# Adding the halves of the value blocks by accumulating transfers, and taking the hidden product in two halves

## What is computed

```python
def swiglu(x, w_in, w_out):
    gate, up = jnp.split(x @ w_in, 2, axis=-1)     # 1024 -> 2 x 2816
    return (jax.nn.silu(gate) * up) @ w_out        # 2816 -> 1024
```

## Time and profile before

| | |
|---|---|
| median of 3 runs | 966.76 us (966.62 to 968.57) |
| the profiled execution's own time | 964.49 us |
| its span, first to last instruction | 962.8 us |
| PE, PEld busy | 99%, 84% of the span |
| DVE, ACT, POOL busy | 88%, 64%, 11% |
| mean granted TensorE clock | 0.998 of full speed |
| DMA, mean over the span | 205 GB/s; SP's queue 55.3%, POOL's 11.1% of the 16 engines |
| chain that ended last | PE 91%, DVE 5%, ACT 2% |

### The profile page before, as it was taken

The page is one execution under the profiler, slowest core; times in us unless marked ns, Lnnn a source line. Parts: engine busy times, 40 slices in busy tenths (PEclk is TensorE's granted clock), DMA queues, the critical chain, the costliest instruction groups (busy, mean ns, idle before and its releaser), DMA issues.

```text
span 962.8 us, 13790 instructions
## 1 busy us (share of the span) xinstructions
PE 952.3 (99%) x4904; PEld 806.8 (84%) x4904; DVE 849.0 (88%) x1174; ACT 620.4 (64%) x727; POOL 108.7 (11%) x146
## 2 busy tenths in 40 slices
PE   9999999999999999999999999999999999999996
PEld 7888888888888888888888888888888888888885
DVE  5999998996898999889889989899898997999886
ACT  6776667436646667675576666549998546667660
POOL 0211111100210111110011101100100100111110
PEclk9999999999999999999999999999999999999999
DMA  9778877753656786876587777935243656786761
GB/s 306 240 228 234 280 235 223 232 178 129 223 180 205 217 244 193 236 227 206 173 237 235 239 231 232 271 124 184 89 131 115 235 192 190 215 242 194 237 162 55
DMA packets 140912, 197.31 MB, mean 205 GB/s; under 512 B 7280, under 2 KB 114336, under 8 KB 140720
## 3 DMA queue, kind: packets, MB, share of 16 engines
q1 hardware_dynamic: 126032, 173.56, 55.3%
q0 software_dynamic: 14256, 22.38, 11.1%
q10 hardware_dynamic: 560, 0.52, 0.2%
HBM read 182.79 MB, written 1.06 MB: 191 GB/s over the span
## 4 chain that ended last, share of the span: by engine, by line
PE 91%; DVE 5%; ACT 2%; issue 1%; DMA 1%; POOL 0%; DVEq 0%; SPq 0%; ACTq 0%
PE psum L2012 23%; PE psum L2026 15%; PE psum L2019 12%; PE psum L1821 12%; PE psum L1830 12%; PE psum L1825 12%; DVE w_lo L995 1%; PE psum L2402 1%; ACT w_hi L503 1%; PE psum L1814 1%; PE psum L2388 1%; DVE w_lo L1031 1%; DMA raw<-in_ffn_w_out 1%; DVE w_lo L1001 1%; PE psum L1996 1%
## 5 line engine op out<-in xcount | busy, mean ns | idle before, releaser
L995 DVE TENSOR_TENSOR w_lo<-raw,w_hi 128x2048 fp32r<-128x2048 f32 x125 | 285.1, 2284 | 20.9 <-ACT w_hi L503 20.8
L2012 PE MATMUL psum<-xT,w_hi 128*128 128x512 f32 x1024 | 254.2, 390 | 0.5
L503 ACT CAST w_hi<-raw 128x2048 fp32r<-128x2048 f32 x125 | 238.3, 1914 | 24.5 <-DMA raw<-in_ffn_w_in 15.0
L2012 PEld LDWEIGHTS psum<-xT,w_hi 128*128 128x128 f32 x1024 | 191.3, 188 | 44.8 <-ACT ffn_tok L573 3.2
L2019 PEld LDWEIGHTS psum<-xT,w_lo 128*128 128x128 f32 x1024 | 139.7, 190 | 10.0
L2019 PE MATMUL psum<-xT,w_lo 128*128 128x256 f32 x1024 | 142.8, 282 | 0.0
L1821 PE MATMUL psum<-w_hi,xT 128*128 128x512 f32 x447 | 128.7, 399 | 0.8 <-DVE arena L1538 0.4
L1830 PE MATMUL psum<-w_hi,xT 128*128 128x512 f32 x447 | 124.8, 390 | 0.2 <-DVE xT L1099 0.2
L1825 PE MATMUL psum<-w_lo,xT 128*128 128x512 f32 x447 | 124.7, 390 | 0.0
L1717 POOL DMA_DIRECT2D ffn_tok<-ffn_tok x64 | 55.0, 859 | 484.7 <-ACT ffn_tok L573 484.7
L1830 PEld LDWEIGHTS psum<-w_hi,xT 128*128 128x128 f32 x447 | 83.9, 188 | 18.3 <-DVE xT L1099 0.5
(11 more groups left out here) (220 smaller groups left out, 1165.3 us busy)
## 6 DMA issues: line engine op xcount, KB each, us to landing
raw<-in_ffn_w_in SPq DMA_DIRECT2D x170, 512.0 KB, 5.2
raw<-in_ffn_w_out SPq DMA_DIRECT2D x88, 512.0 KB, 4.4
raw<-in_c_w_in SPq DMA_DIRECT2D x32, 512.0 KB, 4.7
ffn_tok<-ffn_tok POOLq DMA_DIRECT2D x64, 128.0 KB, 4.9
raw<-in_ab_w_in SPq DMA_DIRECT2D x16, 512.0 KB, 4.9
x_tok<-arena POOLq DMA_DIRECT2D x16, 256.0 KB, 7.3
raw<-in_ab_w_o SPq DMA_DIRECT2D x8, 512.0 KB, 4.2
raw<-in_c_w_o SPq DMA_DIRECT2D x8, 512.0 KB, 4.0
```

Of the source, the lines that this page charges most:

```text
L503: nc.scalar.copy(w_hi[:, slot_of[n]], raw[:, n % RAW]).then_inc(hi_ready, 1)
L995: nc.vector.tensor_tensor(w_lo[:, slot_of[n]], raw[:, n % RAW], w_hi[:, slot_of[n]].bitcast(F32), ALU.subtract).then_inc(lo_ready, 1)
L2012: nc.tensor.matmul(G[0], w_hi[:, slot_of[n + kh], at:at + P], xT_both[:, 4 * kh + k].rearrange("p a s -> p (a s)"), start=kh == k == 0, st ...
```

## The change

`up_add` goes. POOL's `add_gates` becomes `add_halves`: after the transfers for the two gate blocks it issues two more for the value blocks, each once its block is copied out; these have semaphores `value_added[0]` and `value_added[1]`. `up_product` becomes two instructions of 256 columns, one for each block j: it waits for `value_added[j]`. On DVE the first half stays in front of `weight_sums`, the second half and `hidden_sums` come behind them. `hid_product` is two semaphores, so that a copy of block b waits for the half b % 2 alone. On ACT `up_copy(1)` moves ahead of `split_sums_hi` in chunks 4 to 9, and `gates_silu` ahead of `up_copy(3)` in all of them.

```diff
@@ ACT
                 if c > FIRST_FM:
-                    act.wait_ge(hid_product, N_FM * f + c - FIRST_FM)
+                    act.wait_ge(hid_product[b % 2], N_FM * f + c - FIRST_FM)
...
                         hid_early_hi(name, c - 1)
                         hid_late_hi(name, c - 1)
+                        up_copy(name, c, 1)
                         split_sums_hi(name, n)
-                        up_copy(name, c, 1)
                         split_hi(n + 2)
                         up_copy(name, c, 2)
...
                         split_plain_hi(n + 3)
+                    gates_silu(name, c)
                     up_copy(name, c, 3)
-                    gates_silu(name, c)
...
-                act.wait_ge(hid_product, N_FM * (f + 1))
+                for j in range(2):
+                    act.wait_ge(hid_product[j], N_FM * (f + 1))
@@ DVE
-            def up_add(name, c):
-
-                f = SILUS[name]
-                ups = UPS[name]
-                dve.wait_ge(up_copied, 4 * (N_FM * f + c - FIRST_FM + 1))
-                nc.vector.tensor_tensor(ups[:, :, 0:SEQ], ups[:, :, 0:SEQ], ups[:, :, SEQ:], ALU.add
-                                        ).then_inc(up_added, 1)
-
-            def up_product(name, c):
+            def up_product(name, c, j):

                 f = SILUS[name]
-                gates, ups = (a[:, :, 0:SEQ].rearrange("p j (t f) -> p j t f", t=TT) for a in (GATES, UPS[name]))
+                gates, ups = (a[:, j, 0:SEQ].rearrange("p (t f) -> p t f", t=TT) for a in (GATES, UPS[name]))
                 dst = hid_places if c < NC - 2 else hid_blocks[:, 0:512].rearrange("p (j t f) -> p j t f", j=2, t=TT)
                 dve.wait_ge(hidT_lo, NH * f + c)
                 dve.wait_ge(late_lo, N_PROD * f + c)
                 dve.wait_ge(gate_silu, N_FM * f + c - FIRST_FM + 1)
-                dve.wait_ge(up_added, N_FM * f + c - FIRST_FM + 1)
-                nc.vector.tensor_tensor(dst, ups, gates, ALU.mult).then_inc(hid_product, 1)
+                dve.wait_ge(value_added[j], 16 * (N_FM * f + c - FIRST_FM + 1))
+                nc.vector.tensor_tensor(dst[:, j], ups, gates, ALU.mult).then_inc(hid_product[j], 1)
...
                     if c > FIRST_FM:
-                        up_add(name, c - 1)
-                        up_product(name, c - 1)
-                        hidden_sums(name, c - 1)
+                        up_product(name, c - 1, 0)
                     weight_sums(name, n, 0)
                     weight_sums(name, n, 1)
+                    if c > FIRST_FM:
+                        up_product(name, c - 1, 1)
+                        hidden_sums(name, c - 1)
...
                 split_lo(n + 3)
-                up_add(name, last)
-                up_product(name, last)
+                up_product(name, last, 0)
+                up_product(name, last, 1)
@@ POOL (every call of add_gates becomes one of add_halves)
-            def add_gates(name, chunks):
+            def add_halves(name, chunks):
                 for c in chunks:
                     for j in range(2):
                         pool.wait_ge(up_copied, 4 * (N_FM * SILUS[name] + c - FIRST_FM) + j + 1)
                         pool.dma_start(GATES[:, j, 0:SEQ], GATES[:, j, SEQ:], accum_op=ALU.add).then_inc(gate_added[j], 16)
+                    ups = UPS[name]
+                    for j in range(2):
+                        pool.wait_ge(up_copied, 4 * (N_FM * SILUS[name] + c - FIRST_FM) + 2 + j + 1)
+                        pool.dma_start(ups[:, j, 0:SEQ], ups[:, j, SEQ:], accum_op=ALU.add).then_inc(value_added[j], 16)
```

More of the change, by code:

```diff
@@ L150, in build @@
         gate_added = [sem(f"gate_added{j}") for j in range(2)]
-        up_added, x_added = sem("up_added"), [sem(f"x_added{i}") for i in range(4)]
-        gate_silu, hid_product = sem("gate_silu"), sem("hid_product")
+        value_added, x_added = [sem(f"value_added{j}") for j in range(2)], [sem(f"x_added{i}") for i in range(4)]
+        gate_silu, hid_product = sem("gate_silu"), [sem(f"hid_product{j}") for j in range(2)]
         early_used, late_hi, late_lo = sem("early_used"), sem("late_hi"), sem("late_lo")
@@ L1041, in hidden_sums @@
                 else:
-                    dve.wait_ge(hid_product, N_FM * f + c - FIRST_FM + 1)
+                    for j in range(2):
+                        dve.wait_ge(hid_product[j], N_FM * f + c - FIRST_FM + 1)
                 nc.vector.tensor_tensor(s1, a21, a22, ALU.add).then_inc(hid_step1, 1)
@@ L1745, in _ @@
                                ).then_inc(S["pool_tables_landed"], 16)
-                add_gates("F0", (2, 3, 4))
+                add_halves("F0", (2, 3, 4))
                 pool.dma_start(poolw, pool_w[0].rearrange("g p f -> p g f")).then_inc(S["pool_tables_landed"], 16)
-                add_gates("F0", (5,))
+                add_halves("F0", (5,))
                 pool.dma_start(band, consts[:, C_BAND:C_DECAY].rearrange("p (g f) -> p g f", g=4)
                                ).then_inc(S["pool_tables_landed"], 16)
-            add_gates("F0", (6,))
+            add_halves("F0", (6,))
             load_gb(0)
@@ L1773, in _ @@
                     if name == BEFORE_C:
-                        add_gates(name, range(FIRST_FM, 5))
+                        add_halves(name, range(FIRST_FM, 5))
                         pool.wait_ge(S["bound_few"], 1)
@@ L1778, in _ @@
                                            ).then_inc(S["bound_stored"], 16)
-                        add_gates(name, (5,))
+                        add_halves(name, (5,))
                         pool.wait_ge(S["bound_stored"], 16)
@@ L1783, in _ @@
                                            ).then_inc(S["bound_landed"], 16)
-                            add_gates(name, (6 + l,))
-                    add_gates(name, range({"F0": 7, BEFORE_C: 8}.get(name, FIRST_FM), NC - 1))
+                            add_halves(name, (6 + l,))
+                    add_halves(name, range({"F0": 7, BEFORE_C: 8}.get(name, FIRST_FM), NC - 1))
                     add_sums(name)
```

## The result

The changed kernel takes 1003.43 us in the median (1001.36 to 1007.41), the kernel before 966.76 us: a ratio of 1.0378, interval 1.0359 to 1.0398, 36.7 us slower. The forecast was 988.8 us, 22 us slower, with a range of 969 to 1005 us. The direction and the mechanism came out, the size was too small. The profiled execution has a span of 1000.3 us.

The account below looks back on a forecast made before the run. PE was taken to bound the kernel, busy for 952.3 of 962.8 us. Loop 15.4 plus tails 8 less copy 1's 1.4 gave +22 us on the 966.8 us median: 988.8 us, range 969 to 1005.

Parts of the forecast that it names:

- 11.3 + L us: Loop from copy 3 through value transfer, product and hidden sums to PE's products and next copy 3, against a 15.94 us chunk.
- L: Latency from issue to landing of a chunk's last value transfer on POOL's queue; taken as 5.3 us, ends 2.7 and 6.3.
- 20 x 0.77 = 15.4 us: Loss in the loop of chunks 4 to 9: 20 of 24 chunks, 0.7 us each plus 0.1 for PE's restart.
- In chunk 3 ... nothing: Chunk 3 of each block: DVE comes too late anyway and the transfer lands during the weight sums, so no loss.
- The silu ahead of copy 3 ... nothing: ACT's silu before copy 3: the second gate's transfer, issued behind a copy 8 us earlier, is done in time; no cost.
- 2 us in 4 tails, 8 us: Block tails: second half ends 3.5 us later, 1.8 us in hand, some 0.3 more at the norm; 2 us lost each.
- 3/7 of 3.2, so 1.4 us won: Copy 1 ahead of the sums' split: three of PE's seven waits for copies, in chunk 4, go; 1.4 us won.
- The additions taken from DVE: 32 additions, 22.0 us, leave DVE, net 17 us of its work; hidden behind PE, so nothing gained.
- The weight sums: On DVE ahead of the second half product: 2.6 us beside a transfer that takes longer, so they cost nothing.
- R1: Value transfer takes turns with loads instead of queuing behind them: L 4.5, 969 us, or 966 us; chance 0.08.
- R2: Faster: loads are through before the value transfer starts, L is 2.7, all 3.2 us of copy waits go, 963.6 us; chance 0.06.
- R3: Heavier: L is 6.0, all 24 chunks pay 36 us, tails 11 us; +46, 1012 us; chance 0.10.

Follow-up runs that it names:

- e5: The changed kernel with SP holding back each chunk's second weight-unit load (chunks 4 to 9) until value block 1's transfer of two chunks before landed; 985.3 us, ratio 1.0204.
- e2: The changed kernel with both value blocks' halves added on DVE, no value transfers, all new orders kept; 974.3 us, ratio 1.0080.
- v2: The kernel before with one move, ACT's copy 1 ahead of the split of the sums in chunks 4 to 9; 967.4 us, ratio 1.0012.
- e3: The kernel before with 64 more accumulating transfers into bytes nobody reads, no arithmetic waiting for them; 967.0 us, ratio 1.0010.
- e7: The changed kernel with the second half product and the hidden sums in front of the weight sums; 1056.9 us, ratio 1.0945.
- e1: The changed kernel with value block 1's halves added on DVE again, value block 0 still by transfer; 970.5 us, ratio 1.0045.
- v1: e1 with the second half of the product and the hidden sums back in front of the weight sums; 967.2 us, ratio 1.0009.

## Why the prediction was right, and where it was off

**The deciding term.** "11.3 + L us, which only fits into 15.94 us if L is at most 4.6" holds. After the change PE starts 3.35 us + L after copy 3, not 3.25, since DVE starts about 0.1 us behind a landing and the sums take 1.55 with the half product instead of 1.48; the limit is 4.5. L was taken as 5.3 and averages 5.4. The reason given for it, that the load which follows DVE's split comes 1 us ahead of the transfer, is what e5 takes away, and L with it.

**The size, the first error.** "20 x 0.77 = 15.4 us" is for chunks 4 to 9. There 21 waits took 23.0 us, with about 2 us of restarts, and the mean stall is 1.1 us and not 0.7. The limit of 4.5 instead of 4.6 and an L of 5.4 instead of 5.3 each add some 0.1 us. The larger part is the chunks that I left out: "In about 4 of them DVE does table work besides, so that the loads come behind the transfer" did not come true, since chunks 5, 6 and 7 of F0, beside the table work, all wait. All 24 chunks at 5.4 - 4.5 = 0.9 us give 21.6 us, most of the 23.0. Scatter of L adds little.

And "In chunk 3 ... nothing" is wrong: all four chunks 3 wait, 3.5 us together. This is the order's price, 5.1 us in e2 without a transfer. The step that failed there was to let the hidden sums' 1.7 us of delay be set off by the earlier copy 0. "The silu ahead of copy 3 ... nothing" is wrong in chunk 2, where ACT comes to copy 3 without slack: the row of 2.6 us among the waits after.

**The tails, the second error.** "2 us in 4 tails, 8 us" measured 10.4 us of waits and 9.2 us of time, in three tails: F3's has no loads of a next block, its last transfer lands in 2.7 us and PE has no such wait. That the sum came out near is partly luck, three tails at 3 us instead of four at 2, and the path was not the one forecast. I followed DVE's lo part (L1271 before); PE waited for ACT's hi part behind a split whose load was late, and for DVE's hidden product.

**Copy 1.** "3/7 of 3.2, so 1.4 us won" failed by itself: v2 measured 1.2 us lost. The forecast read three waits for copy 1 where there are two, 0.9 us together, and when these went the time did not. In the changed kernel the waits at copies 0 and 1 went as well, but that comes with the first half product too.

**What cost nothing.** The additions taken from DVE brought nothing by themselves (forecast: nothing). The traffic of 64 transfers cost nothing that can be told (e3). The weight sums were a cover, worth 53 us once there is a transfer to cover (e7, against 1003.4).

**The rivals.** R1 and R2 needed an L of 4.5 or less, and L averages 5.4 us against 2.6 us with no load in front. The Trainium skill (DMA: Bandwidth & Descriptors, Queues, rings and completion order) says that a DMA engine takes turns between its queues, a packet at a time. I read that as a mild delay, as in R1; the average of 5.4 us does not bear this out. R3 is nearest in size, in part by another way: L is not 6.0 on average, but as R3 has it all of chunks 4 to 9 pay on average, and chunk 3 pays besides.

## What to carry to other kernels

A slack of 4.6 us against a latency of 2.7 us looks safe, but a transfer's latency belongs to its place in the traffic: ask what was issued just ahead of it, and whether the change itself moves that. An addition of 0.4 us on an engine with time to spare is cheaper than a transfer, if the result stands in the loop that PE closes; the gates' transfers are harmless because ACT needs them some 7 us later. Where a new order of work is a cover for a wait, price it without the wait too: here it cost 3.3 us by itself (e1 against v1), and all the new orders together 8 us (e2).

## What the runs showed of the hardware

In e2 PE stood idle for 2.7 us before 124.8 us. Its busy times by stretch (columns: length, then busy us and instructions of PE, PEld, DVE, ACT, POOL, the granted clock, DMA share, GB/s):

```profile
118.00:121.00 3.00, 3.00 (x18) 2.65 (x17) 2.93 (x5) 0.00 (x0) 0.00 (x0) 1.00 1.08 367
...
124.80:128.00 3.20, 3.20 (x8) 2.52 (x9) 2.60 (x2) 0.88 (x2) 0.88 (x1) 0.50 0.86 277
```

After that gap the granted clock was 0.50, the 1.2 GHz level, and 8 matmuls took 3.67 us, where they take 1.98 us at the upper level: a loss of 1.7 us beyond the gap itself. The gap's length alone does not decide this. In the changed kernel a wait of 2.4 us ahead of 383.8 us was followed by the full clock, and in e3's tail waits of at most 1.9 us were followed by 0.50 for 3 us. First the changed kernel, then e3, with the same columns:

```profile
383.80:386.00 2.20, 2.20 (x10) 1.82 (x11) 2.20 (x2) 2.20 (x3) 0.86 (x1) 1.00 0.08 32
```

```profile
623.40:626.40 3.00, 3.00 (x8) 2.30 (x7) 2.73 (x3) 0.89 (x1) 0.00 (x0) 0.50 0.53 113
```

The mean clock of the changed kernel's profiled execution is 0.998, as before, so none of the 37.5 us between the two spans comes from there. Its four other executions had 0.993 to 0.997, where those of the kernel before had 0.997 to 0.999, so a small part of its median may.
